# Feed-forward layers split into groups of 384, 448 and 256 tokens, with one product for both halves of x in the last group

## The reference

```
x += 0.5 * swiglu_ffn(x, ffn1...)
x += mixer(rmsnorm(x))            # RG-LRU branch and gated linear attention
x += cross_attention(rmsnorm(x))  # 256 memory tokens
x += 0.5 * swiglu_ffn(x, ffn2...)
y  = rmsnorm(x)

def swiglu_ffn(x, g, w_gate, w_up, w_down):
    h = rmsnorm(x, g)
    return (jax.nn.silu(h @ w_gate) * (h @ w_up)) @ w_down
```

## Time and profile before

| | |
|---|---|
| median of 3 runs | 2378.79 us (2378.36 to 2382.55) |
| profiled execution, its own time as its span | 2379.0 us |
| PE busy | 2343.7 us, 99% of the span, 14996 products |
| PEld busy | 2285.3 us |
| DVE busy | 1062.5 us, 45% |
| POOL busy | 519.1 us, 22% |
| ACT busy | 494.6 us, 21% |
| mean granted PE clock | 0.995 of full speed |
| HBM traffic | 280.54 MB read, 70.72 MB written |

### The profile page before, as it was taken

One profiled execution on the slowest core, in us unless ns is written; L12 is line 12 of the kernel. 1 busy time (PEld: TensorE's weight loads), 2 busy tenths in 40 slices (PEclk: granted clock), 3 DMA queues, 4 the chain that ended last, 5 costly groups with the idle time before them and its releaser, 6 DMA issues. The chain is left out here.

```text
span 2379.0 us, 36652 instructions
## 1 busy us (share of the span) xinstructions
PE 2343.7 (99%) x14996; PEld 2285.3 (96%) x14996; DVE 1062.5 (45%) x1696; ACT 494.6 (21%) x697; POOL 519.1 (22%) x239
## 2 busy tenths in 40 slices
PE   7999999999999999999999999999999999999998
PEld 7999999999999989899889999799999999999998
DVE  6434334444334574565642423444443344443345
ACT  4222212122211241321410221331111011111101
POOL 2444334344432000000001000022221222221121
PEclk9999999999999999999999999999999999999999
DMA  4554454454452465666678376731101010111112
GB/s 158 213 212 168 159 194 175 151 212 168 159 194 89 156 214 182 212 222 240 231 261 316 145 254 252 276 110 54 53 36 53 35 53 35 53 35 53 35 36 76
DMA packets 89475, 352.50 MB, mean 148 GB/s; under 512 B 8944, under 2 KB 16432, under 8 KB 79152
## 3 DMA queue, kind: packets, MB, share of 16 engines
q1 hardware_dynamic: 89104, 351.12, 40.3%
q10 hardware_dynamic: 288, 0.18, 0.0%
HBM read 280.54 MB, written 70.72 MB: 148 GB/s over the span
## 5 line engine op out<-in xcount | busy, mean ns | idle before, releaser
L1736 PE MATMUL ps<-a_hi,w_sb 128*128 128x384 f32 (+1 forms) x2112 | 691.6, 327 | 6.6 <-DVE a_lo L1227 4.6
L1738 PE MATMUL ps<-a_hi,w_sb 128*128 128x384 f32 (+1 forms) x2112 | 689.9, 327 | 0.0
L1737 PE MATMUL ps<-a_lo,w_sb 128*128 128x384 f32 (+1 forms) x2112 | 689.7, 327 | 0.0
L696 POOL TENSOR_TENSOR w_sb<-w_raw,w_sb 128x1024 fp32r<-128x1024 f32 x132 | 317.7, 2415 | 1066.4 <-ACT w_sb L772 1066.4
L1736 PEld LDWEIGHTS ps<-a_hi,w_sb 128*128 128x128 f32 x2112 | 397.7, 188 | 8.3 <-issue 3.5
L1737 PEld LDWEIGHTS ps<-a_lo,w_sb 128*128 128x128 f32 x2112 | 397.8, 188 | 0.0
L1738 PEld LDWEIGHTS ps<-a_hi,w_sb 128*128 128x128 f32 x2112 | 397.6, 188 | 0.0
L1310 DVE SCALAR_TENSOR_TENSOR x<-ps,x 128x384 f32<-128x384 f32 (+1 forms) x528 | 279.2, 534 | 199.7 <-PE ps L1738 199.7
L1296 DVE TENSOR_TENSOR hf<-sil,ps 128x384 f32<-128x384 f32 x132 | 70.1, 531 | 646.9 <-ACT sil L849 646.9
L1736 PE MATMUL ps<-h_hi,w_sb 128*128 128x384 f32 (+1 forms) x1056 | 344.7, 326 | 0.0
L1738 PE MATMUL ps<-h_hi,w_sb 128*128 128x384 f32 (+1 forms) x1056 | 344.2, 326 | 0.0
(11 more groups left out here) (262 smaller groups left out, 2717.2 us busy)
## 6 DMA issues: line engine op xcount, KB each, us to landing
w_sb<-split SPq DMA_DIRECT2D x148, 1024.0 KB, 5.2
split<-st_w SPq DMA_DIRECT2D x60, 1024.0 KB, 4.1
st_raw<-in_mix_tiles SPq DMA_DIRECT2D x60, 512.0 KB, 5.9
w_raw<-in_ffn_gate SPq DMA_DIRECT2D x44, 512.0 KB, 3.6
w_raw<-in_ffn_up SPq DMA_DIRECT2D x44, 512.0 KB, 4.4
w_raw<-in_ffn_down SPq DMA_DIRECT2D x44, 512.0 KB, 4.3
kc<-in_cache_k SPq DMA_DIRECT2D x5, 1024.0 KB, 8.5
kc<-in_cache_v SPq DMA_DIRECT2D x4, 1024.0 KB, 9.6
```

The lines of the kernel that those rows point to most:

```text
L696: nc.gpsimd.tensor_tensor(w_lo_sb[:, slot_, :], raw[:, slot_, :], w_hi_sb[:, slot_, :].bitcast(F32), ALU.subtract)\
L1736: nc.tensor.matmul(dst, w_h, x_h, start=start, stop=False)
L1737: nc.tensor.matmul(dst, w_h, x_l, start=False, stop=False)
L1738: return nc.tensor.matmul(dst, w_l, x_h, start=False, stop=stop)
```

## The change

The two feed-forwards and the final norm use groups of their own: `FNS` = 384, 448, 256 tokens in place of 384, 384, 320. The mixer and the cross-attention keep the old groups. In the third group (256 tokens) the normed halves x_hi and x_lo lie in one tile `a_both`, and gate and up use `joint_mm`: w_hi by both halves at once, 512 columns into a whole bank, and w_lo by x_hi, 256 columns, into its first half. Behind the step ACT copies the second halves of gate's and up's banks into `part`, DVE adds the first halves from PSUM to them into `whole`, ACT takes silu from `whole`, and DVE multiplies `sil` by `whole`. `part` and `whole` lie in the place of `sq`. Down stays as it was, with the new group widths. The norm of group 1 of the second feed-forward now covers tokens of the old group 2, so its first quad waits for four tiles of that group's `co`, and its sum on DVE moves from behind the fifth to behind the seventh eviction. `w_al` and `w_a2` have new places.

```diff
+
+
+FOFFS = [0, 384, 832]
+FNS = [384, 448, 256]
+FMAX = 448
...
         a_hi, a_lo = [None] * 3, [None] * 3
-        for n in range(3):
-            a_hi[n], o = at(f"a_hi{n}", [P, KT, NS[n]], o, F32R)
-            a_lo[n], o = at(f"a_lo{n}", [P, KT, NS[n]], o, F32R)
+        for n in range(2):
+            a_hi[n], o = at(f"a_hi{n}", [P, KT, FNS[n]], o, F32R)
+            a_lo[n], o = at(f"a_lo{n}", [P, KT, FNS[n]], o, F32R)
+        a_both, o = at("a_both", [P, 2, KT, FNS[2]], o, F32R)
+        a_hi[2], a_lo[2] = a_both[:, 0], a_both[:, 1]
...
             elif kind == "ffn2":
-                eng.wait_ge(evicted, FIRST["co", n] + 8)
+                eng.wait_ge(evicted, FIRST["co", min(n + 1, 2) if n else 0] + (4 if n == 1 else 8))
...
                         wait_source(act, kind, n)
+                    elif (kind, n) == ("ffn2", 1):
+                        act.wait_ge(evicted, FIRST["co", 2] + 8)
...
-                    N = NS[n]
-                    nc.scalar.activation(sil[:, s % 2, 0:N], ps[:, 4 + 2 * (s % 2), 0:N], ACT.Silu).then_inc(silu_done, 1)
+                    N = FNS[n]
+                    b = 4 + 2 * (s % 2)
+                    if n == 2:
+                        ft, _ = ffn_step(first, s)
+                        nc.scalar.activation(part[:, :, :], ps[:, b:b + 2, N:2 * N], ACT.Copy).then_inc(part_out, 1)
+                        act.wait_ge(whole_out, f * 2 * ITS + q0 // 6 * 2 + ft + 1)
+                        nc.scalar.activation(sil[:, s % 2, 0:N], whole[:, 0, :], ACT.Silu).then_inc(silu_done, 1)
+                    else:
+                        nc.scalar.activation(sil[:, s % 2, 0:N], ps[:, b, 0:N], ACT.Silu).then_inc(silu_done, 1)
...
                         b = 4 + 2 * (s % 2)
+                        if n == 2:
+                            dve.wait_ge(part_out, f * 2 * ITS + 2 * it + ft + 1)
+                            nc.vector.tensor_tensor(whole[:, :, :], part[:, :, :], ps[:, b:b + 2, 0:N], ALU.add).then_inc(whole_out, 1)
                         dve.wait_ge(silu_done, G + q0 + s + 1)
                         if f or not first or s >= 2:
                             dve.wait_ge(hid_done, G + q0 + s - 1)
-                        nc.vector.tensor_tensor(hf[:, s % 2, 0:N], sil[:, s % 2, 0:N], ps[:, b + 1, 0:N], ALU.mult).then_inc(h_done, 1)
+                        up = whole[:, 1, :] if n == 2 else ps[:, b + 1, 0:N]
+                        nc.vector.tensor_tensor(hf[:, s % 2, 0:N], sil[:, s % 2, 0:N], up, ALU.mult).then_inc(h_done, 1)
...
                 norm_rows(*beside)
                 for j in range(8):
                     evict("co", n, j)
-                    if n == 2 and j == 4:
+                    if n == 2 and j == 6:
                         norm_sum("ffn2", 1, 0)
...
+            def joint_mm(dst, w_h, w_l, x_both, start, stop):
+
+                N = x_both.shape[2]
+                nc.tensor.matmul(dst[:, 0:2 * N].rearrange("p (a n) -> p a n", a=2), w_h, x_both, start=start, stop=False)
+                return nc.tensor.matmul(dst[:, 0:N], w_l, x_both[:, 0], start=False, stop=stop)
...
+                                b = 4 + 2 * (s % 2) + u
+                                if n == 2:
+                                    ins = joint_mm(ps[:, b, :], w_hi_sb[:, w, c], w_lo_sb[:, w, c], a_both[:, :, k, :], k == 0, k == KT - 1)
+                                else:
+                                    ins = split_mm(ps[:, b, 0:FNS[n]], w_hi_sb[:, w, c], w_lo_sb[:, w, c],
+                                                   a_hi[n][:, k, :], a_lo[n][:, k, :], k == 0, k == KT - 1)
```

63 lines of the change are left out of this document (34 added, 29 removed).

## The result

The changed kernel takes 2400.18 us (2396.70 to 2404.63, 4 runs); the kernel before, run beside it, 2380.67 us (2378.36 to 2382.84, 4 runs). The ratio is 1.0085, 95% interval 1.0071 to 1.0100: slower by some 20 us, where 2377.0 and no change were forecast and 2382.5 was the top of the range. Five more executions of the changed kernel in a later measurement gave 2399.53 us.

What follows compares the result with a forecast made beforehand. TensorE, busy practically the whole 2379.0 us, was taken as the bound. -9.4 us for the joint product, +2.3 and +2.3 up to and around each feed-forward's first iteration, +0.8 and +2.0 at their ends gave -2.0: 2377.0 us, range 2371.0 to 2382.5.

Steps and rivals of the forecast that it cites:

- A product costs 13.3 ns however long it is.: All TensorE products: time is columns/2.4 GHz plus a fixed 13.3 ns, read from four lengths.
- a fixed cost that mostly isn't one per product: Gate and up: only a fifth of the fixed cost saved, 2384.6 us; chance 0.02.
- The joint product saves: Gate and up of both feed-forwards: one fixed cost less per slice and weight tile, 704 x 13.3 ns = -9.4 us.
- Rival 3: Gate and up: the joint product takes 2 x 120 ns and saves nothing, 2386.4 us; chance 0.04.
- Middle iterations: Sixth step before down: copy and addition of the halves stay hidden within 4.16 us of slack, cost 0.
- Rival 2: Down in 20 middle iterations: the sixth step's chain exceeds 4.16 us; slower, 2417 if POOL held the multiply; chance 0.10.
- First iterations: Sixth step of each feed-forward's first iteration: GpSimd holds the multiply, delaying down; +1.75 us in the first, +1.5 in the second.
- The pairs' waits of 0.8 us: First iterations: TensorE's wait for a third-group pair of `a_lo` goes away, -0.8 us twice.
- Start: Kernel start: longer load of `x` and longer square of group 1 delay the first `a_hi`, +0.95 us.
- Last cross-attention tiles: Before the second feed-forward: the later `norm_sum` meets GpSimd's work and delays the last `co` eviction, +0.9 us.
- End of the first feed-forward: VectorE sets the pace from the second group's end, so the third group's shorter down is no gain; +0.8 us.
- Tail: Kernel end: shorter down lost under GpSimd's chain, with longer sums and squares there; +2.0 us.

Runs made afterwards that it cites:

- the sum in PSUM: Changed kernel, but the addition writes the halves' sum back into the PSUM banks, where SiLU and the multiply read it; 2396.11 us, ratio 1.0063.

## Why the prediction was wrong, point by point

- **"A product costs 13.3 ns however long it is." This step failed.** It rested on four lengths, 256, 320, 384 and 512, none of them the new one. At 448 the cost beyond the columns is 19.9 ns: 3168 products x 6.6 ns = **+20.9 us**, in place of 0. Alone this turns -2.0 into +18.9, and the median rose by 19.5. The series of 448 columns alone, the groups without the joint product (25 us slower than the kernel before), and an iteration's products alone (71.57 us) show it three ways. That the two differences agree within 1 us is partly luck: the profiled executions lie 23.8 us apart, and the other terms were off both ways. I gave 0.02 to "a fixed cost that mostly isn't one per product", for the opposite reason.
- The joint product saves: right in kind. 360.0 to 347.0 ns in the middle iterations, 704 x 13.0 = -9.2 us, expected -9.4; without it an iteration takes 71.98 us, with it 71.57. Rival 3 (2 x 120 ns) is out. By the Trainium skill ("TensorE: Matmul & The Clock Gate", section "Wait — 56ns, not 53.3ns?"), 2.5 ns a product, it would by estimate have been -1.8; the trace disagrees, with 13.0 ns saved for each joint product.
- Middle iterations: right, 0. Rival 2 didn't occur; no wait there.
- First iterations: the mechanism was right, the multiply with two SBUF operands waits for GpSimd, 2.00 and 2.19 us (the sum in PSUM shows it). Its size was off: with all its terms I had the first iterations longer by 0.9 and 1.0 us; they were by 3.8 and 3.7 in one execution, by 2.8 and 0.1 in another, 0.9 of it the slow length. What I left out is a second catch, of `h_lo`, decided by 0.1 us, the slower products behind the wait, and a wait of 0.5 us for `hf` in the first feed-forward. The 0.1 is flattered by the clock, 0.98 there and 0.96 in the kernel before.
- The pairs' waits of 0.8 us went, as said. Start: +1.0 against +0.95. Last cross-attention tiles, with the mixer: +2.0 against 0.9, but 1.7 of it is the clock in the mixer; the wait on `x L1407` is 1.2, and was 0.6 before, so this term was too large. End of the first feed-forward: +1.2 against +0.8, of which 0.3 is the slow length. Tail: +3.3 against +2.0, of which 0.3 is the slow length; TensorE now waits for GpSimd's sums three times (0.7, 0.6 and 1.1 us), before once (1.6), and 1.9 instead of 1.4 for VectorE's `st`.
